# Five-step normalisations with VectorE adding the squares, and a new order of two streams at their seams

## The reference, cut to what matters

```
def rms_norm_2(x, g):
    xf = x.astype(jnp.float32)
    y = xf * lax.rsqrt(jnp.mean(xf * xf, axis=-1, keepdims=True) + NORM_EPS)
    return (y * g.astype(jnp.float32)).astype(x.dtype)

h = modulate(rms_norm_2(x, g), mod[..., j, :], mod[..., j + 1, :])    # h * (1 + scale) + shift
gt, up = jnp.split(h @ w_up, 2, axis=-1)
x = x + 0.5 * mod[..., j + 2, :] * ((silu(gt) * up) @ w_down)
```

## Time and profile before

| | before |
|---|---|
| median of 3 runs | 2731.35 us (2729.72 to 2733.39) |
| the profiled execution | 2730.26 us, span 2728.5 us |
| mean granted TensorE clock | 0.929 |
| PE busy | 2489.5 us (91%), 20772 instructions |
| PE weight loads busy | 2416.0 us (89%) |
| DVE busy | 1627.5 us (60%), 2686 instructions |
| ACT busy | 983.9 us (36%) |
| POOL busy | 180.6 us (7%), 300 instructions |
| DMA | 352.82 MB, mean 129 GB/s |

### The profile page before, as it was taken

One profiled execution on the slowest core, in us unless ns is written; L12 is line 12 of the kernel. 1 busy time (PEld: TensorE's weight loads), 2 busy tenths in 40 slices (PEclk: granted clock), 3 DMA queues, 4 the chain that ended last, 5 costly groups with the idle time before them and its releaser, 6 DMA issues.

```text
span 2728.5 us, 48201 instructions
## 1 busy us (share of the span) xinstructions
PE 2489.5 (91%) x20772; PEld 2416.0 (89%) x20772; DVE 1627.5 (60%) x2686; ACT 983.9 (36%) x1441; POOL 180.6 (7%) x300
## 2 busy tenths in 40 slices
PE   6779988799969999988789899999999999867999
PEld 6779988699969999988668899999999998856999
DVE  5648878378857777743583777764333334355554
ACT  5336545255522222221273332223222223134443
POOL 0000000071000000000000720000000000100000
PEclk9779989599969999988899899998999998879899
DMA  6225654056625555521101355542233232201454
GB/s 227 85 64 192 241 184 155 16 167 241 202 83 187 198 193 196 187 73 59 39 1 47 128 196 193 196 153 70 96 99 99 96 100 72 77 16 39 148 193 162
DMA packets 104020, 352.82 MB, mean 129 GB/s; under 512 B 18816, under 2 KB 18944, under 8 KB 103424
## 3 DMA queue, kind: packets, MB, share of 16 engines
q1 hardware_dynamic: 95616, 348.94, 37.4%
q0 software_dynamic: 8192, 0.80, 0.3%
HBM read 348.63 MB, written 1.05 MB: 128 GB/s over the span
## 4 chain that ended last, share of the span: by engine, by line
PE 60%; issue 6%; DVE 3%; ACT 1%; POOL 1%; POOLq 0%; DVEq 0%; ACTq 0%
PE slot L833 18%; PE slot L834 17%; PE slot L835 17%; PE slot L895 2%; PE slot L980 1%; PE slot L873 1%; PE slot L971 1%; ACT PTSA L1406 1%; POOL R0B L734 1%; PE slot L884 1%; PE slot L861 1%; PE slot L864 1%; PE slot L863 1%; DVE PRA L1861 0%; PE slot L962 0%
## 5 line engine op out<-in xcount | busy, mean ns | idle before, releaser
L1644 DVE TENSOR_TENSOR W_lo<-W_raw,W_hi 128x1024 fp32r<-128x1024 f32 x510 | 623.1, 1224 | 708.7 <-ACT W_hi L1302 702.9
L1302 ACT ACTIVATE W_hi<-W_raw 128x1024 fp32r<-128x1024 f32 x510 | 539.7, 1061 | 1186.0 <-PE slot L835 1050.0
L833 PE MATMUL slot<-H_hiA,W_lo 128*128 128x256 f32 x2864 | 813.5, 284 | 22.7 <-DVE VA L2067 6.5
L834 PE MATMUL slot<-H_loA,W_hi 128*128 128x256 f32 x2864 | 806.5, 282 | 0.0
L835 PE MATMUL slot<-H_hiA,W_hi 128*128 128x256 f32 x2864 | 805.7, 281 | 0.0
L833 PEld LDWEIGHTS slot<-H_hiA,W_lo 128*128 128x128 f32 x2864 | 553.4, 193 | 31.4 <-issue 16.4
L834 PEld LDWEIGHTS slot<-H_loA,W_hi 128*128 128x128 f32 x2864 | 553.8, 193 | 0.0
L835 PEld LDWEIGHTS slot<-H_hiA,W_hi 128*128 128x128 f32 x2864 | 553.0, 193 | 0.0
L833 PE MATMUL slot<-H_hiB,W_lo 128*128 128x256 f32 x1280 | 357.2, 279 | 4.4 <-DVE VB L2067 4.4
L834 PE MATMUL slot<-H_loB,W_hi 128*128 128x256 f32 x1280 | 356.2, 278 | 0.0
L835 PE MATMUL slot<-H_hiB,W_hi 128*128 128x256 f32 x1280 | 355.9, 278 | 0.0
(11 more groups left out here) (258 smaller groups left out, 3270.8 us busy)
## 6 DMA issues: line engine op xcount, KB each, us to landing
W_raw<-wstream SPq DMA_DIRECT2D x510, 512.0 KB, 3.9
A_raw<-adastream SPq DMA_DIRECT2D x144, 512.0 KB, 3.5
BT<-par POOLq DMA_DIRECT2D x256, 3.0 KB, 2.6
CON<-const SPq DMA_DIRECT2D x1, 1025.5 KB, 8.0
XA<-xT SPq DMA_DIRECT2D x2, 512.0 KB, 4.5
SC<-cond SPq DMA_DIRECT2D x1, 1024.0 KB, 15.2
XB<-ctxT SPq DMA_DIRECT2D x1, 1024.0 KB, 16.7
PAR<-par SPq DMA_DIRECT2D x1, 684.0 KB, 9.3
```

The source lines that it names most:

```text
L833: pe.matmul(out, wl, xh, start=start, stop=False, skip_group_check=True)
L834: pe.matmul(out, wh, xl, start=False, stop=False, skip_group_check=True)
L1302: act.activation(W_hi[:, g % HIGH, :], W_raw[:, g % RAW, :], ACT.Copy).then_inc(S.w_hi, 1)
L1644: dve.tensor_tensor(W_lo[:, g % RAW, :], W_raw[:, g % RAW, :], W_hi[:, g % HIGH, :].bitcast(F32), ALU.subtract).then_inc(S.w_lo, 1)
```

## The change

A normalisation gets five steps instead of four, and `final` four instead of three. In step 0 DVE, after its update, adds the squared tiles: tiles 0, 1 and 2, 3 in one addition of 128x512, the two results in one of 128x256, and tiles 4, 5 and tiles 6, 7 in one of 128x256 each. The sum over the features on PE moves to step 1 and takes 6 matmuls instead of 16. The spread moves to step 2, scaling to steps 3 and 4. ACT's squares stay in step 0, POOL's root and DVE's `rstd` in step 1. `b_may` gets a rule: steps 1 and 2 of a norm of B wait until A has left its norm and stands at step 1 or 2 of the next stage. With it the order at a joint seam is A n0, B y, A n1, B z, A n2, B n0, A n3, A n4, A u0, B n1, A u1, B n2, A u2, B n3, B n4, B u0, A u3, B u1; at seam 5, where the first units are A's alone, A u3 comes before B n4.

```diff
     def norm(s, solo, blk, which, l, old):
-        add(s, "norm", [G, G, G, G], solo, dict(tok=1, upd=1 if old else 0, sq=3, rs=1, sc=8, hr=8), l=l,
+        add(s, "norm", [G] * 5, solo, dict(tok=1, upd=1 if old else 0, sq=3, rs=1, sc=8, hr=8, nm=1), l=l,
             blk=blk, which=which, old=old)
...
-    add("A", "final", [G, G, G], True, dict(tok=1, upd=1, sq=3, rs=1), blk=1, old=old)
+    add("A", "final", [G] * 4, True, dict(tok=1, upd=1, sq=3, rs=1, nm=1), blk=1, old=old)
...
         u = b[ib].unit
         if u is None:
+            v = b[ib]
+            if v.stage.kind == "norm" and v.i in (1, 2) and ia < len(a):
+                return a[ia].stage.kind != "norm" and a[ia].i >= v.i
             return True
...
             def norm_sums(s, st):
                 open_token(s, st, st.tok)
                 p = ps(st, st.tok)
-                for i, (a, b) in enumerate(((0, 4), (4, 6), (6, 8))):
-                    pe.wait_ge(s.sem.squared, st.sq + i + 1)
-                    for kt in range(a, b):
-                        for tt in range(2):
-                            mm = pe.matmul(p[:, 0, tt:tt + 1], s.SQ[kt // 4][:, kt % 4, P * tt:P * tt + P],
-                                           con("ones", 1), start=kt == 0 and tt == 0, stop=kt == KT - 1,
-                                           skip_group_check=True)
+                for i, kt in enumerate((0, 4, 6)):
+                    pe.wait_ge(s.sem.summed, 3 * st.nm + i + 1)
+                    for tt in range(2):
+                        mm = pe.matmul(p[:, 0, tt:tt + 1], s.SQ[kt // 4][:, kt % 4, P * tt:P * tt + P],
+                                       con("ones", 1), start=i == 0 and tt == 0, stop=i == 2, skip_group_check=True)
                 mm.then_inc(s.sem.stats, 1)
...
             def norm(s, st):
+                yield
                 norm_sums(s, st)
                 yield
                 norm_spread(s, st)
...
+            def add_squares(s, st):
+
+                a, b = s.SQ
+                dve.wait_ge(s.sem.squared, st.sq + 1)
+                step(dve.tensor_tensor(a[:, 0:2, :], a[:, 0:2, :], a[:, 2:4, :], ALU.add))
+                dve.tensor_tensor(a[:, 0, :], a[:, 0, :], a[:, 1, :], ALU.add).then_inc(s.sem.summed, 1)
+                for i in range(2):
+                    dve.wait_ge(s.sem.squared, st.sq + 2 + i)
+                    dve.tensor_tensor(b[:, 2 * i, :], b[:, 2 * i, :], b[:, 2 * i + 1, :], ALU.add)\
+                       .then_inc(s.sem.summed, 1)
+
             def norm(s, st):
                 tok = st.tok
                 p = ps(st, tok)
                 finish_update(s, st)
+                add_squares(s, st)
                 yield
 
                 rstd(s, st, st.rs, p[:, 0, 0:2], 2, D, EPS)
+                yield
                 yield
```

More of the change, by code:

```diff
@@ L154, in __init__ @@
         self.qk = count["qk"]
+        self.nm = count["nm"]
 class Old:
@@ L169, in make_streams @@
 def make_streams():
-    count = {s: dict(tok=0, v=0, upd=0, sq=0, rs=0, sc=0, hr=0, pair=0, grp=0, qk=0) for s in "AB"}
+    count = {s: dict(tok=0, v=0, upd=0, sq=0, rs=0, sc=0, hr=0, pair=0, grp=0, qk=0, nm=0) for s in "AB"}
     stages = dict(A=[], B=[])
@@ L456, in __init__ @@
         self.squared = new("squared" + s)
+        self.summed = new("summed" + s)
         self.stats = new("stats" + s)
```

## The result

The changed kernel takes 2773.5 us (median of four executions, 2760.9 to 2788.0) against 2730.5 for the kernel before on the same chip (2727.8 to 2733.4). The ratio is 1.0135, 95% interval [1.0097, 1.0174]. The change makes the kernel slower. The forecast of 2751 had the direction, but the time lies 22 us above it and above its range.

What follows compares the result with a forecast made beforehand. PE, busy 91% of the span, was taken to bound the kernel. Seam 3's loss of 45 less 22.1 from four seams and 3.5 from normalisations with A alone gave +19.4 us: median 2751, range 2738 to 2765.

Steps and rivals of the forecast that it cites:

- In feed-forwards nothing changes: Feed-forward stages: time there is PE's and the change touches nothing in them, so no term was given.
- The sum: Whole kernel: 45 lost at seam 3, less 22.1 from four other seams and 3.5 from normalisations with A alone: +19.4 us.
- The stall: Seam 3: the context's root queues behind the bias table's 128 DMA issues, PE idle some 51 us; loss 45 us (41 to 47).
- Rival 2: Seam 3: the table does not hold the context's root back, so the kernel is faster; 2701 if not held at all; chance 0.07.
- The normalisations with A alone: Normalisations without the context: start gains 3.0, two before first-network feed-forwards lose 0.25 each, last gains 1.0; together 3.5 us gain.
- The gain of seams 1 to 4: Joint seams: A u3 starts earlier, gaining 7.0 us at seam 1, 3.6 at seam 2, 4.5 at seam 4; seam 3 loses.
- S + 21.5: Seam 4: forecast start of A u3, counted from S, the start of scaling A; range S + 19.8 to S + 24.2.
- two shorter pauses instead of one long one: Joint seams, worked out at seam 4: the new order's PE pauses, used to place A u3 between full-speed and low-clock ends.
- Seam 5: First four units are A's, so no wait for their weights; gain 7 us (5.0 to 9.3).
- The additions: Each normalisation: adding squared tiles costs DVE 1.9 us; sums leave 12 records instead of 32, 1.4 or 2.6 us on PE.
- Rival 1: Joint seams: PE's low clock takes nearly all that they give; +32 us, time 2764; chance 0.17.
- Rival 3: Seams all at the high clock and seam 3's first DMA following its memset at once; +7 us, time 2739; chance 0.13.

Runs made afterwards that it cites:

- experiment 10: Changed kernel without the new `b_may` rule, PE waiting before most of the image's tokens in shared feed-forwards until its previous token left its bank: 2905.5 us, ratio 1.0623.
- experiment 5: The changed kernel again, nothing edited, beside the kernel before in a second comparison on one chip: 2760.6 us against 2736.9, ratio 1.0103.
- Experiments 1 and 2: 1: changed kernel, second bias table issued four units later, 2718.9 us. 2: kernel before, only the context's root at seam 3 moved behind the table, 2786.7 us.
- Experiment 7: Changed kernel with the second bias table later and, at seams 1 to 4, A u3's weight converted ahead of the context's scaling: 2700.3 us, ratio 0.9866.
- experiment 4: Changed kernel with five steps and rule kept, but without DVE's additions, so 32 records for each sum as before: 2793.8 us, ratio 1.016.
- experiments 3 and 8: Both: changed kernel without the new `b_may` rule, five steps and additions kept. First run 2691.3 us, ratio 0.9808; repeat in a third comparison 2703.3 us, ratio 0.9879.

## Why the prediction was right or wrong

**The step that failed** is "In feed-forwards nothing changes", and with it that the sum is made against one profiled execution's own time. The sum took that execution's paces for the kernel's. PE has two paces at the full clock, 0.1133 and 0.1178 us a matmul. In the shared feed-forwards and the last one it takes one or the other when it starts again after a pause (experiment 10), and with no extra matmul in the row it kept it for the whole row in every profile. In the twelve profiles without made pauses seven of the 36 shared feed-forwards were slow, and three of the twelve last ones. The profile of before happened to have none, that of after three of four: 34.3 us between them that no run ties to either kernel. The medians fit that: they are 43.0 us apart in the first comparison and 23.7 in that of experiment 5, where both kernels ran again. That the median of 2773.5 lies above the range and not in it is, by this, in good part luck: the 2760.6 of the second comparison would lie in it. Two paces appear in no term and in no rival of the prediction. There the clock was the only thing that could change PE's speed.

**The sum, at equal pace**, is +23.4 where +19.4 was forecast. The mark is the start of the 73rd matmul from A u3's first on (for seam 5 of the unit that stands in its place), when PE is back at the full clock in either kernel, less the excess up to there. Before it stands at 815.5, 1197.9, 1535.5, 1915.0 and 2300.1, after at 807.9, 1186.5, 1570.1, 1945.4 and 2325.4. Behind the stroke is the second profile of the changed kernel:

| stretch | forecast | measured |
|---|---|---|
| start to seam 1 | -3.0 + 2 x 0.25 - 7.0 = -9.5 | -7.6 / -5.1 |
| seam 2 | -3.6 | -3.8 / -3.3 |
| seam 3 | +45 | +46.0 / +45.3 |
| seam 4 | -4.5 | -4.2 / -4.3 |
| seam 5 | -7.0 | -5.1 / -5.1 |
| the rest | -1.0 | -1.9 / -3.2 |

- **The stall** is right in its place, cause and size: root of the context at 1566.5 for 1564.8, 50.4 us of idle PE for 51, a loss of 46.0 for 45. Experiments 1 and 2 show it from both sides: 55.7 us come back when the table moves (the stall, and the gain that the seam itself then has) and 48.2 are lost when only the root moves. Rival 2 is refuted. On the issuing side the trace does not agree with the Trainium skill ("DMA: Bandwidth & Descriptors", Anatomy of one DMA), which calls descriptor generation on this path small: 128 issues took 61.08 / 128 = 0.477 us each, and POOL's next instruction stood behind them. What POOL spends that time on no run shows.
- **The normalisations with A alone** were mis-sized, and with them the stretch up to seam 1 (2 to 4 us). The start gives its 3.0: the first unit begins at 25.25 instead of 28.28. But the first unit behind the fourth normalisation begins at 566.78, and at 570.56 in the second profile, against 566.32 before; with the excess taken off that is 565 to 567 against 565. Of the 2.5 us forecast nothing is left there. What took it back is not shown.
- **The gain of seams 1 to 4** has two errors that cancel. The wait for A u3's weight was counted as time, but not the low clock behind it, 1.6 us: "two shorter pauses instead of one long one" were three. And S + 21.5 was too late for the start of A u3, which came at S + 20.0 to 20.9. Experiment 7 takes wait and low clock away together and gains 10.7.
- **Seam 5** lacked a term behind B u0. B u0 started at S + 19.9, near the early end of its range. But ACT's squares of the image's first projected tiles (`SQ2A`) were not ready when it was done, and PE, which went on without a wait there before (2295.57), waited 2.08 us and then met the low clock. From the first matmul of B u0 to the 73rd it took 15.95 us, 3.8 more than the 12.15 of before. So some 9 us were gained up to B u0, where 7 were forecast, and 3.8 lost behind it. The wait stands in all six profiles with the rule of the order (1.68 us in experiment 4, 2.07 or 2.08 in the others) and in none without it. PE's row:

```profile
2345.94 1.92 PE L880 MATMUL slot<-CON,SQ2A 128*128 128x2 f32 x16 [2.08 <-ACT SQ2A L1568]
```

- **The additions** cost 1.9 us of DVE as worked out, and they carry the gain: 21.2 us in the changed kernel (experiment 4). The prediction gave no separate value for them at the joint seams, so it did not see that the rule brings nothing beside them, and as it stands costs 9 to 11 us. With the table out of the way, the five steps, additions and the old order come to 2681.9 and 2680.1, with the rule to 2690.7, and with the rule and the earlier conversion to 2680.0.
- **Rival 1** (the low clock takes nearly all) has not happened: seams 2, 4 and 5 gave 3.3 to 5.1 us. Its 2764 lies nearer to the median for another reason. **Rival 3** was refuted by the stall of 46 and by the low clock at each seam.

What stays open is what decides the pace. The same program draws differently in another execution where it starts after a pause. In the shared feed-forwards about one start in five is slow, but the row of 336 or 360 matmuls that ends ahead of seam 3 is slow in 8 of 13 profiles, so the odds are not the same everywhere. One small matmul mostly changes nothing, and twelve between B y and B z always left the slow pace. This looks like a matter of rhythm between matmuls and something that runs beside them, but no run here shows what. Nor do the runs exclude that an order of work shifts the odds.

## What to carry to other kernels

Where one engine walks through a common order, look up what each step issues on every queue before it is moved. Here three lines of order put a root of 0.7 us behind 61 us of DMA issues and turned a gain of 32 us into a loss of 23, and nothing but the place of the table had to change. Before a span is compared with another, count the matmuls in equal windows of the long stretches at the full clock: if they differ, part of the difference is not the edit's. And a wait of PE costs its length and the low clock behind it, so price both.

## What the hardware showed

- Two paces of PE at the full granted clock: 0.1133 and 0.1178 us from one 128x256 matmul to the next (179 and 173 in a window of 20 us). The slow pace lasted for up to 3,130 matmuls in a row. Behind pauses of 3.2 to 6.1 us 6 of 27 rows were slow, and behind 12 records of one column between B y and B z, with no pause, 36 of 36. One extra matmul of one column inside a row left the pace as it was in 64 of 66 places and ended the slow pace in two.
- Executions of one unchanged kernel spread over 40 us (2723.7 to 2763.7 in seventeen), 1.5%. In the two pairs of profiles of one kernel (experiments 3 and 8, and the changed kernel's) the spans differ by 16.0 and 29.6 us and their excess by 17.8 and 30.6.
- A matmul of one column on 32-bit operands inside a row of 256-column ones costs 0.25 us (22.01 us for 192 and one extra, 21.76 for 192).
- After waits of 2.1 to 2.7 us PE did 12 to 16 matmuls at 0.213 us before it was back at the full clock.
- GpSimd's 128 issues of a small DMA took 61 us, 0.477 us each, and its next instruction stood behind them.
